# Two sets of transposes moved from TensorE to VectorE's 32x32 squares: the convolution's z and the mix branches' y

## The reference, cut to what matters

```python
def _conv_mixer(h, w_in, conv_w, conv_b, w_out):
    bg, cg, v, g = jnp.split(h @ w_in, 4, axis=-1)
    y = bg * _dwconv3(cg * v, conv_w, conv_b)
    return (y * jax.nn.silu(g)) @ w_out
```

```python
y_a = diff_attention(qa, ka, va, lam, lam_init, a_subln[l])     # [256, 512]
y_b = chunk_attention(qb, kb, vb, b_rel_bias[l])                # [256, 512]
y_c = retention(qc, kc, vc, cg, c_out_norm[l])                  # [256, 512]
merged = (g[:, :, 0] * (y_a @ w_branch_a[l]) + g[:, :, 1] * (y_b @ w_branch_b[l])
          + g[:, :, 2] * (y_c @ w_branch_c[l]))
x = x + merged @ w_out[l]
```

## Time and profile before

| | |
|---|---|
| median of 3 runs | 1900.0 us (1899.23 to 1900.65) |
| the profiled execution, measured | 1901.5 us |
| its span, first to last instruction | 1899.5 us |
| TensorE busy | 1878.0 us, 99% |
| TensorE's mean granted clock | 0.998 |
| GpSimd busy | 1362.4 us, 72% |
| ScalarE busy | 917.1 us, 48% |
| VectorE busy | 783.7 us, 41% |

### The profile page before, as it was taken

How to read it: one execution, slowest core, us unless ns; L and a number is a source line. 1 busy time by engine, 2 the same in 40 slices (tenths; PEclk the granted TensorE clock), 3 DMA queues, 4 the chain that set the end, 5 groups by cost and what they waited for, 6 DMA issues and landing times.

```text
span 1899.5 us, 25192 instructions
## 1 busy us (share of the span) xinstructions
PE 1878.0 (99%) x9578; PEld 1521.1 (80%) x9578; DVE 783.7 (41%) x1445; ACT 917.1 (48%) x1365; POOL 1362.4 (72%) x568
## 2 busy tenths in 40 slices
PE   6999999999999999999999999999999999999999
PEld 3779777887787888888788888888888878888887
DVE  4313511675543342575540432433166564043253
ACT  3314521676354564455555454455445555546442
POOL 2523344346876789879678988888887967898886
PEclk9999999999999999999999999999999999999999
DMA  9662576437768377656556566657765655656663
GB/s 357 226 234 66 157 272 214 115 98 264 245 211 297 124 223 218 192 178 188 152 150 185 185 188 191 195 168 224 214 194 169 197 152 146 187 177 197 191 191 130
DMA packets 194840, 363.97 MB, mean 192 GB/s; under 512 B 32260, under 2 KB 48372, under 8 KB 194164
## 3 DMA queue, kind: packets, MB, share of 16 engines
q1 hardware_dynamic: 191280, 351.72, 58.8%
q10 hardware_dynamic: 3460, 10.88, 1.7%
HBM read 361.50 MB, written 6.10 MB: 194 GB/s over the span
## 4 chain that ended last, share of the span: by engine, by line
PE 96%; DMA 1%; DVE 1%; ACT 1%; SPq 1%; ACTq 0%; issue 0%; POOL 0%
PE ps L1140 27%; PE ps L1142 27%; PE ps L1141 27%; PE ps L1158 2%; PE ps L1364 2%; PE ps L1830 1%; PE ps L1828 1%; PE ps L1829 1%; PE ps L1744 1%; PE ps L1185 1%; PE ps L1516 1%; PE ps L1487 1%; DMA proj<-in_ada_w 1%; PE ps L1497 1%; PE ps L1789 1%; PE ps L1166 1%
## 5 line engine op out<-in xcount | busy, mean ns | idle before, releaser
L514 POOL TENSOR_TENSOR w_lo<-raw,w_hi 128x1024 fp32r<-128x1024 f32 x556 | 1343.4, 2448 | 487.8 <-ACT w_hi L552 464.6
L552 ACT ACTIVATE w_hi<-raw 128x1024 fp32r<-128x1024 f32 x556 | 572.4, 1059 | 428.2 <-DMA raw<-in_ffn_w_up 100.1
L1140 PE MATMUL ps<-w_hi,xt_hi 128*128 128x512 f32 (+1 forms) x1952 | 757.6, 388 | 5.1 <-POOL w_lo L514 3.8
L1142 PE MATMUL ps<-w_hi,xt_lo 128*128 128x512 f32 (+1 forms) x1952 | 744.6, 381 | 0.0
L1141 PE MATMUL ps<-w_lo,xt_hi 128*128 128x512 f32 (+1 forms) x1952 | 744.1, 381 | 0.0
L1140 PEld LDWEIGHTS ps<-w_hi,xt_hi 128*128 128x128 f32 x1952 | 367.4, 188 | 96.4 <-issue 25.6
L1142 PEld LDWEIGHTS ps<-w_hi,xt_lo 128*128 128x128 f32 x1952 | 367.3, 188 | 71.8
L1141 PEld LDWEIGHTS ps<-w_lo,xt_hi 128*128 128x128 f32 x1952 | 367.8, 188 | 66.1
L2335 DVE STREAM_TRANSPOSE ps<-proj 32x256 f32<-32x256 f32 (+1 forms) x384 | 166.5, 434 | 6.5
L1140 PE MATMUL ps<-w_hi,xt_hi_ctx 128*128 128x512 f32 (+1 forms) x432 | 169.0, 391 | 0.2
L1142 PE MATMUL ps<-w_hi,xt_lo_ctx 128*128 128x512 f32 (+1 forms) x432 | 166.7, 386 | 0.0
(11 more groups left out here) (225 smaller groups left out, 1575.8 us busy)
## 6 DMA issues: line engine op xcount, KB each, us to landing
raw<-in_w_in SPq DMA_DIRECT2D x120, 512.0 KB, 3.8
raw<-in_ffn_w_gate SPq DMA_DIRECT2D x88, 512.0 KB, 4.4
raw<-in_ffn_w_up SPq DMA_DIRECT2D x88, 512.0 KB, 4.4
raw<-in_ffn_w_down SPq DMA_DIRECT2D x88, 512.0 KB, 4.3
pt<-in_ada_w SPq DMA_DIRECT2D x44, 512.0 KB, 4.9
raw<-in_pool_w_in SPq DMA_DIRECT2D x32, 512.0 KB, 7.6
raw<-in_na_w_in SPq DMA_DIRECT2D x32, 512.0 KB, 4.7
raw<-in_conv_w_in SPq DMA_DIRECT2D x32, 512.0 KB, 5.8
```

What stands on the lines that cost most here:

```text
L514: pool.tensor_tensor(w_lo[:, s, :], raw[:, s, :], w_hi[:, s, :].bitcast(F32), ALU.subtract).then_inc(lo_done, 1)
L552: act.activation(w_hi[:, g % SLOTS, :], raw[:, g % SLOTS, :], ACT.Copy).then_inc(hi_done, 1)
L1140: pe.matmul(o, h, hi, start=start, stop=False)
L1142: return pe.matmul(o, c, hi, start=False, stop=stop)
```

## The change

TensorE no longer turns z and y, and ScalarE no longer copies z. VectorE turns both with a new helper, 16 instructions a set. One set does half of z (four feature chunks by two tiles of rows) straight into the padded buffer in SBUF, or the whole y of one branch into the same two PSUM banks as before. `z_turned(0)` stands right behind `z_made(1)`, `z_turned(1)` right behind `z_made(3)` and ahead of `taps(0)`. `y_turned(0)` and `y_turned(2)` stand behind the two `y_normed`. The readers wait for VectorE in place of TensorE. TensorE waits for the low parts of both branches ahead of the branch products instead of holding the banks as turned.

```diff
@@ scalar, conv_layer
-                def turned_z(k):
-                    act.wait_ge(pe_done, pe_s.count(("tp", "cvz", 0, k)))
-                    act.wait_ge(dve_done, dve_s.count("cv_pad"))
-                    act.activation(free(proj[:, 0:1], [[ZT_ROW, 2], [1, SEQ]], ZT + 2 * k * ZT_ROW + 1),
-                                   ps[:, CV_Z_BANK[k], :].rearrange("p (c n) -> p c n", c=2), ACT.Copy).then_inc(act_done, act_s.one(("zt", k)))
...
-                    if n in (2, 4):
-                        turned_z(n - 2)
-                        turned_z(n - 1)
@@ scalar, mix, y_high
-                        act.wait_ge(pe_done, pe_s.count(("tp", f"y{br}{l}", 0, k)))
+                        act.wait_ge(dve_done, dve_s.count(("tp", f"y{br}{l}")))
@@ tensor, conv_layer
-                def turn_z(k):
-                    pe.wait_ge(acc_free[(b + k // 2 * 2 + 1) % 2], reads(b + k // 2 * 2 + 1))
-                    turn("cvz", 0, k, lambda t, c: pj(D + (2 * k + c) * P, P, NA_COLS, t=t), (act_s, ("zt", k)), bank=CV_Z_BANK[k])
...
-                between = {2: lambda: (turn_z(0), turn_z(1)), 4: lambda: (turn_z(2), turn_z(3)), 7: lambda: (turn_p(0), turn_p(1))}
+                between = {7: lambda: (turn_p(0), turn_p(1))}
@@ tensor, mix
-                def turn_y(br):
...
-                    for br in (0, 2):
-                        if G == MIX_Y[br][0]:
-                            turn_y(br)
...
+                        for k in range(2):
+                            pe.wait_ge(dve_done, dve_s.count(("xt", f"y{2 - 2 * j}{l}", 0, k)))
@@ vector
+            def squares_turned(to, rows):
+                for i in range(4):
+                    for q in range(4):
+                        last = dve.transpose(to(q, 32 * i), rows(i, 32 * q))
+                return last
@@ vector, conv_layer
+                def z_turned(h):
+                    dve.wait_ge(acc_free[(b + 2 * h + 1) % 2], reads(b + 2 * h + 1))
+                    squares_turned(
+                        lambda q, n: free(proj[32 * q:32 * q + 32, 0:1], [[ZT_ROW, 4], [P, NT], [1, 32]], ZT + 4 * h * ZT_ROW + 1 + n),
+                        lambda i, n: free(proj[32 * i:32 * i + 32, 0:1], [[P, 4], [NA_COLS, NT], [1, 32]], D + h * 512 + n))\
+                        .then_inc(dve_done, dve_s.one(("zt", h)))
...
-                    dve.wait_ge(act_done, act_s.count(("zt", k)))
+                    dve.wait_ge(dve_done, dve_s.count(("zt", k // 2)))
...
                 z_made(1)
+                z_turned(0)
                 ada_beside("cv_in", 2)
                 copied(2)
                 ada_beside("cv_in", 3)
                 z_made(3)
+                z_turned(1)
                 taps(0)
@@ vector, mix
+                def y_turned(br, col):
+                    dve.wait_ge(dve_done, dve_s.count(("y", l, br)))
+                    dve.wait_ge(act_done, act_s.count(("apt0", l, MIX_SOFT - 1)))
+                    squares_turned(lambda q, n: free(ps[32 * q:32 * q + 32, MIX_Y[br][1], 0:1], [[SEQ, 4], [P, NT], [1, 32]], n),
+                                   lambda i, n: free(proj[32 * i:32 * i + 32, 0:1], [[P, 4], [IN_COLS, NT], [1, 32]], col + n))\
+                        .then_inc(dve_done, dve_s.one(("tp", f"y{br}{l}")))
...
                 y_normed(2, BQ, Y_STAT + 8)
+                y_turned(0, AQ)
+                y_turned(2, BQ)
                 y_low(0)
```

## The result

| | before | after |
|---|---|---|
| median of 7 runs each | 1899.13 us | 1906.85 us |
| ratio, 95% interval | | 1.0046 (1.0036 to 1.0056) |
| span of the profiled execution | 1899.5 us | 1903.7 us |
| TensorE busy | 1878.0 us | 1873.8 us |
| TensorE's mean granted clock | 0.998 | 0.996 |

What follows compares the result with a forecast made beforehand. TensorE, busy 99% of the span, was taken to bound the kernel; -5.2 transposes, +0.8 and +9.9 stalls and +3.0 clock gave +8.5 us, so 1908.5 us after allowing for the profiled run's 1.5 us; range 1899 to 1912.

Steps and rivals of the forecast that it cites:

- 5.2 us off TensorE: Six places with 8 transposes, 0.87 us each, leave TensorE: 1.74 us in the convolution, 3.48 in the mix layers.
- Squares as in the feed-forward stage, 7.5 us a set: VectorE's 16 squares of 32x256 take 7.5 us a set, bounded for z between 3.8 and 8 us.
- Rival 3: Squares into SBUF take the shared port and wait for low parts in the convolution: 1920 to 1930 us, chance 0.06.
- First set costs 0: Convolution: the modulation's sums, copied behind z's first set, are ready at 487.5, wanted at 487.66; bound 0 to 0.5 us.
- copied(4) ends at 528.45, stall 0.8: Convolution block 6: VectorE's copied(4) comes after TensorE is ready at 527.76, a stall of 0.8 us.
- GpSimd restarts at 530.0 and makes 7 low parts to 547.4: Convolution, block 6: GpSimd makes 7 low parts until its 8 slots are used up; seven taps pass with them.
- Copy done at 550.0, turn wanted at 540.2, stall 9.9: Convolution block 6: TensorE waits 9.9 us for VectorE's copy of the modulation's sums before turning them.
- Clock 3.0: After TensorE's idle stretch in block 6 its clock drops to half speed, costing 3 us, bounded 0 to 3.4.
- Sum +8.5: Whole kernel: -5.2 + 0.8 + 9.9 + 3.0 us, giving 1908.5 us; this case 1904 to 1910.5, chance 0.70.
- Rival 1: Convolution: all VectorE work covered, TensorE loses only transposes, -5.2 us, 1894.8 us; chance 0.13.
- Rival 2: Convolution: half of the taps pass, VectorE some 2 us ahead at 530.0, stall 5 us; +1.3, 1901 us, chance 0.11.
- one tap per low part: Convolution: beside back-to-back GpSimd instructions, one VectorE tap passes for each low part of 2.4 us.

Runs made afterwards that it cites:

- the kernel that kept TensorE busy: Changed kernel plus 36 matmuls into a free bank ahead of TensorE's wait at the block 6 turn of the modulation's sums: 1904.97 us, ratio 1.0029.
- the doubled set: Changed kernel with the second set of z's squares made twice on VectorE, ahead of the taps: 1907.78 us, ratio to the kernel before 1.0046.

## Why the prediction was right

Point by point, with the 2.7 us of offset added to the times of after:

- **5.2 us off TensorE**: 5.3 us were measured where nothing else gets in the way (taps in PSUM). Of this the mix layers' 3.5 were 3.8 by the ratio and 3.6 (twice 1.79) by the rows.
- **Squares as in the feed-forward stage, 7.5 us a set**: 7.19 from SBUF to SBUF (0.44 each, also while GpSimd ran), 15.03 for the two of y. Rival 3, the squares taking the port, falls with this row.
- **First set costs 0**: right; the copy began at 483.87 and there is no wait of note. The kernel with the first set alone has 4.2 of 4.35 us.
- **copied(4) ends at 528.45, stall 0.8**: it ended at 525.53, with the offset 528.2; stall 0.52.
- **GpSimd restarts at 530.0 and makes 7 low parts to 547.4**: 527.16 and 544.36, with the offset 529.9 and 547.1, 7 of them.
- **Copy done at 550.0, turn wanted at 540.2, stall 9.9**: 549.6, 540.2 and 9.41. This term was right within 5%, and it carries the sign. It was a bottleneck that could not be read from shares of busy time: VectorE rose from 41% to 44%.
- **Clock 3.0**: this term was too large, 2.2 in the profile and 2.5 by the kernel that kept TensorE busy. I took nearly the whole of the start's 3.4, but part of the 10.2 us at half speed fell into the idle time itself.
- **Sum +8.5**: 7.7 by the medians, 8.7 by the ratio, 6.9 by the account of the profile. The three losses were 0.3, 0.5 and 0.8 too large there, all to the same side. The upper bound of this case comes to 1910.2 from its terms, not 1910.5; nothing rests on it.

Rival 1 (all covered) is what the kernel would be if the taps did not take the port: 1894.8 was its price, 1893.1 the version with the taps in PSUM. Its doubt in the prediction, that the queue of 14 us of bare work fits only if no tap waits, was the right one. Rival 2 fell: VectorE was not 2 us ahead at the restart of GpSimd, and seven taps waited there, as many as the stepping has. A half way does exist for another order of the queue (2.7 us with the sums ahead of the last taps).

What stays open: why TensorE's wait at block 6 differs between executions (0.5 and 1.0 us for the same queue), and what sets the end of the stall. The changed kernel fits the count of slots, but no run has another number of them, and the doubled set came to the same end with gaps in GpSimd's run.

## What to carry to other kernels

Before work is moved to an engine that is idle half the time, look at what stands behind it in that engine's queue and at what shares a port with it: 7 us of squares cost 12 us (0.5 + 9.4 + 2.2), because they pushed seven taps beside the other engine's back-to-back run, where each took some 2.5 us in place of 0.45. A running sum that VectorE kept in a free PSUM bank took the taps out of that wait: 0.48 to 0.54 us each beside GpSimd. And where instructions wait for another engine's run, their number beside it counts, not the sum of the work: 7 us more squares cost nothing measurable, another order of the queue won back 6 of 8.7 us, and only leaving out the second set or taking the taps off the shared port removed the loss.

## What was not expected of the hardware

**The wait for GpSimd is not always for one instruction.** Two executions of different kernels, in a stage where no instruction differs, reach the same product of 128x512 with two SBUF inputs at almost the same point of GpSimd's run. First the kernel with y alone, VectorE and GpSimd:

```profile
655.73 1.69 DVE L2702 TENSOR_TENSOR proj<-x_res,qt 128x512 f32<-128x512 f32 x1
```

```profile
652.10 10.39 POOL L514 TENSOR_TENSOR w_lo<-raw,w_hi 128x1024 fp32r<-128x1024 f32 x4
```

Then the kernel with the first set and y:

```profile
655.66 6.40 DVE L2703 TENSOR_TENSOR proj<-x_res,qt 128x512 f32<-128x512 f32 x1
```

```profile
652.05 9.46 POOL L514 TENSOR_TENSOR w_lo<-raw,w_hi 128x1024 fp32r<-128x1024 f32 x4
```

And the stretch behind it, with busy times and the granted clock as above:

```profile
663.40:670.30 6.90, 6.12 (x18) 4.90 (x18) 6.63 (x15) 4.73 (x16) 0.00 (x0) 0.51 0.63 172
```

In the second, VectorE let two further low parts go first and got its turn only when GpSimd had nothing more to do. TensorE then waited 1.9 us for it and ran at half clock for 6.9 us. The profiled execution took 1900.4 us, in a kernel whose median is 1894.9. The kernel with the sums ahead of the last taps has the same product at 6.40 us too, until 669.28, while GpSimd's run ends at 668.73:

```profile
662.88 6.40 DVE L2686 TENSOR_TENSOR proj<-x_res,qt 128x512 f32<-128x512 f32 x1
```

TensorE waits 1.9 us for it there as well. These two profiled executions are each the slowest of their ten, so part of the scatter of such a kernel may be this; that is not shown. In the kernel before a product of 4 columns is of the same kind. It ends at 494.74, where GpSimd's run of 8 ends (494.71 in the earlier trace rows):

```profile
489.61 5.13 DVE L1916 TENSOR_TENSOR mods<-ada_sums,cols 128x4 f32<-128x4 f32 x1
```

I read it as chance in who gets the port next; why it falls one way or the other is open. So "one tap per low part", on which the prediction rests, held for every tap of the changed kernel that met GpSimd's run, but it is the common case and not the most that such an instruction can cost.

**Short idle stretches cost clock.** Idle TensorE for 0.5 us at block 6 of the changed kernel left the clock at 1.00, and so did 1.0 us in the kernel with z alone. Behind the 1.9 us above it was 0.51. 2.6 us there in the doubled kernel brought it down:

```profile
526.90:533.60 6.70, 6.07 (x14) 4.79 (x15) 6.67 (x4) 3.18 (x3) 6.63 (x3) 0.50 0.40 148
```

6.7 us at half speed lose some 3 us, more than the wait itself. In the doubled kernel they were not paid on top, since TensorE had to wait at the turn of the sums in any case (4.2 us in place of 9.4).
